# Sums of squares on GpSimd, half slabs of the context first, 64-row filter tiles and re-spread side slabs in a two-block fp32 kernel

## The reference, cut to what matters

```python
def rmsnorm(x, g):                        # ten norms of this kind, over the 1024 features
    xf = x.astype(jnp.float32)
    xf = xf * lax.rsqrt(jnp.mean(xf * xf, axis=-1, keepdims=True) + NORM_EPS)
    return xf.astype(x.dtype) * g
...
x = x + jnp.concatenate([y_attn, y_ssd, y_pool], axis=-1) @ w_out
h = rmsnorm(x, norm_ffn)
gate, up = jnp.split(h @ w_gate_up, 2, axis=-1)
return x + (jax.nn.silu(gate) * up) @ w_down            # then rmsnorm(x, norm_final)
...
def ffn_half(s, shift, scale, gate, g_pre, g_post, w_in, w_out):
    h = swiglu(modulate(rmsnorm_2(s, g_pre), shift, scale), w_in, w_out)
    return s + 0.5 * gate * rmsnorm_2(h, g_post)
...
# hyena_kernel: the filter net on 64 features, then (256x64) @ (64x2048), times a decay
h = jnp.sin(freq * (z @ w1 + b1))
h = jnp.sin(freq * (h @ w2 + b2))
h = jnp.sin(freq * (h @ w3 + b3))
h = (h @ w4).astype(f32)
```

## Time and profile before

| | us |
|---|---|
| median of 3 runs (lowest, highest) | 1420.91 (1420.67, 1421.95) |
| the profiled execution, whole | 1422.07 |
| its span in the trace | 1420.2 |
| PE busy in the span | 1321.3 |
| DVE, ACT, POOL busy | 865.0, 590.7, 58.1 |

### The profile page before, as it was taken

One profiled execution on the slowest core, in us unless ns is written; L12 is line 12 of the kernel. 1 busy time (PEld: TensorE's weight loads), 2 busy tenths in 40 slices (PEclk: granted clock), 3 DMA queues, 4 the chain that ended last, 5 costly groups with the idle time before them and its releaser, 6 DMA issues.

```text
span 1420.2 us, 20572 instructions
## 1 busy us (share of the span) xinstructions
PE 1321.3 (93%) x8392; PEld 1175.9 (83%) x8392; DVE 865.0 (61%) x1360; ACT 590.7 (42%) x942; POOL 58.1 (4%) x68
## 2 busy tenths in 40 slices
PE   6898799999699999999989899999899988899996
PEld 6887799998588888888766798778588987899996
DVE  4775677696878765554324794347766664555544
ACT  5564445444423232222213552236335634444542
POOL 0040000000000000000001430001000000000000
PEclk9999999999799999999989999999999998899998
DMA  6343277675355675566223153223223443355552
GB/s 253 121 148 119 96 233 225 208 240 177 124 186 192 191 230 194 181 203 204 83 78 111 53 167 108 89 96 128 74 75 100 143 152 127 106 188 182 173 173 71
DMA packets 60510, 213.02 MB, mean 150 GB/s; under 512 B 6608, under 2 KB 8784, under 8 KB 60160
## 3 DMA queue, kind: packets, MB, share of 16 engines
q1 hardware_dynamic: 58880, 205.55, 44.4%
q0 software_dynamic: 1248, 5.44, 1.1%
q10 hardware_dynamic: 288, 0.71, 0.1%
HBM read 210.63 MB, written 1.05 MB: 149 GB/s over the span
## 4 chain that ended last, share of the span: by engine, by line
PE 80%; DVE 10%; ACT 5%; issue 3%; DMA 1%; SPq 0%; POOLq 0%; POOL 0%; DVEq 0%; ACTq 0%
PE ps L1573 23%; PE ps L1575 22%; PE ps L1574 22%; ACT hi L482 3%; PE ps L1618 3%; DVE lo L962 2%; PE ps L1922 1%; PE ps L1609 1%; PE ps L1610 1%; PE ps L1611 1%; PE ps L1973 1%; PE ps L1886 1%; DVE rinv L984 1%; PE ps L1962 1%; PE ps L1941 1%
## 5 line engine op out<-in xcount | busy, mean ns | idle before, releaser
L1573 PE MATMUL ps<-nh,hi 128*128 128x256 f32 (+1 forms) x1936 | 611.6, 316 | 40.7 <-DVE lo L962 14.3
L962 DVE TENSOR_TENSOR lo<-raw,hi 128x1024 fp32r<-128x1024 f32 (+1 forms) x322 | 390.1, 1212 | 376.8 <-ACT hi L482 376.7
L1574 PE MATMUL ps<-nh,lo 128*128 128x256 f32 (+1 forms) x1936 | 599.0, 309 | 0.0
L1575 PE MATMUL ps<-nl,hi 128*128 128x256 f32 (+1 forms) x1936 | 598.8, 309 | 0.0
L482 ACT ACTIVATE hi<-raw 128x1024 fp32r<-128x1024 f32 (+1 forms) x322 | 334.6, 1040 | 504.9 <-PE ps L1575 469.1
L1573 PEld LDWEIGHTS ps<-nh,hi 128*128 128x128 f32 x1936 | 376.2, 194 | 75.4 <-issue 26.6
L1574 PEld LDWEIGHTS ps<-nh,lo 128*128 128x128 f32 x1936 | 377.2, 195 | 17.5 <-issue 0.5
L1575 PEld LDWEIGHTS ps<-nl,hi 128*128 128x128 f32 x1936 | 376.5, 194 | 16.3
L1573 PE MATMUL ps<-H,hi 128*128 128x256 f32 (+1 forms) x528 | 174.7, 331 | 0.3 <-DVE lo L962 0.3
L1574 PE MATMUL ps<-H,lo 128*128 128x256 f32 (+1 forms) x528 | 169.0, 320 | 0.0
L1575 PE MATMUL ps<-H,hi 128*128 128x256 f32 (+1 forms) x528 | 168.9, 320 | 0.0
(11 more groups left out here) (292 smaller groups left out, 991.5 us busy)
## 6 DMA issues: line engine op xcount, KB each, us to landing
raw<-in_up SPq DMA_DIRECT2D x132, 512.0 KB, 3.5
raw<-in_in SPq DMA_DIRECT2D x86, 512.0 KB, 3.3
raw<-in_w_ada SPq DMA_DIRECT2D x72, 512.0 KB, 4.2
raw<-in_down SPq DMA_DIRECT2D x48, 512.0 KB, 3.8
raw<-in_down SPq DMA_DIRECT2D x24, 384.0 KB, 3.1
raw<-in_out SPq DMA_DIRECT2D x8, 512.0 KB, 3.3
raw<-in_hy_out SPq DMA_DIRECT2D x8, 512.0 KB, 3.3
raw<-in_da_out SPq DMA_DIRECT2D x8, 512.0 KB, 3.3
```

The costliest lines, as they stand in the source:

```text
L962: dve.tensor_tensor(lo[:, h, 0:w], raw[:, r, 0:w], hi[:, h, 0:w].bitcast(F32), ALU.subtract).then_inc(lo_done, 1)
L1573: mm(o, hi[:, h, wk], x_hi, start=first, stop=False)
L1574: mm(o, lo[:, h, wk], x_hi, start=False, stop=False)
L1575: return mm(o, hi[:, h, wk], x_lo, start=False, stop=last)
```

## The change

- `TURNS` gets a semaphore `acc`. GpSimd's new `gather` adds the squares of tiles 0 to 6 or 0 to 7 of a norm, one 128x256 (or 128x512) addition for each tile after the first; PE then does one product with ones (`gathered`), and in most norms a second for the last tile (`last_square`), in place of eight. This holds for mix1, ffn1, pre2c, pre2x, post2, mod2c, post_mix2 and post3 (38 additions 256 wide, 12 of 512); mod2x and pre3 keep eight products. ACT's wait ahead of a square is now for `acc`. The places of the products move: mix1's behind slab 1 of in1, mod2c's to one place behind slab 7 of mixed, ffn1's and post_mix2's ahead of the last tile of their stage's last slab, pre2x's, post2's and post3's behind slab 22.
- The first three slabs of up2 are gone through twice on PE: first the context's 256 columns of all three, then those of x (`half_product`). The context's operands (pre2c) are made four slabs earlier in down1.
- The filter net's third layer is computed twice, on partitions 0 to 63 and 64 to 127; `w4` comes in one DMA of 128 rows, and the two products of a block take rows 0 to 63 and 64 to 127. The blocks stand behind slabs 13, 15, 18 and 20 of down2, their sums behind 15, 17, 20 and 22. In down2 ACT does `down_pair` ahead of `split`.
- `rides`: 12 in up1, 4 in down1, none in up2 until slab 6, then one behind each, two behind slabs 30 to 35, 12 in down2.
- The second half of x's load goes behind the first weight slab. In in1 many small steps move by a slab or so on all engines, and four of the small products become two. V's copies are shared by ACT and DVE, and PE waits for them later. In da_out, o2, out1, down1 and down3 the order of a `split` and the norm's steps beside it is turned round on ACT or DVE at the last slab.

The diff, cut to its core:

```diff
 TURNS = {
+    "acc": dict(mix1=6, ffn1=6, pre2c=7, pre2x=6, post2=6, mod2c=7, post_mix2=6, post3=6),
-    "stat": dict(mix1=8, ffn1=8, pre2c=8, pre2x=8, post2=8, mod2x=8, mod2c=8, post_mix2=8, pre3=8, post3=8),
+    "stat": dict(mix1=1, ffn1=1, pre2c=1, pre2x=1, post2=1, mod2x=8, mod2c=1, post_mix2=1, pre3=8, post3=1),
...
+            def gather(m, tiles, to, per=1):
+                for k in range(1, TURNS["acc"][m] + 1):
+                    pool.wait_ge(sem("sq"), since("sq", m) + per * (k + 1))
+                    if k > 1:
+                        pool.wait_ge(sem("acc"), since("acc", m) + k - 1)
+                    pool.tensor_tensor(to, tiles(0) if k == 1 else to, tiles(k), ALU.add)\
+                        .then_inc(sem("acc"), 1)
...
                 if k >= 4:
-                    act.wait_ge(sem("stat"), since("stat", m) + k - 3)
+                    if m in TURNS["acc"]:
+                        act.wait_ge(sem("acc"), since("acc", m) + max(1, k - 4))
...
             for x in st["o2"]:
-                split(x.s + HL)
                 down_one("post_mix2", x)
+                if x.j < KD - 1:
+                    split(x.s + HL)
             root("post_mix2")
+            split(x.s + HL)
...
             for x in st["down2"]:
-                split(x.s + HL)
                 if x.last:
                     down_pair(x)
-                if x.j in (14, 16, 18, 20):
-                    magnitudes((x.j - 14) // 2)
+                split(x.s + HL)
+                if x.j in (14, 16, 19, 21):
+                    magnitudes((14, 16, 19, 21).index(x.j))
...
+            def gathered(m, acc, o):
+                pe.wait_ge(sem("acc"), since("acc", m) + TURNS["acc"][m])
+                return mm(o, ones, acc, start=True, stop=TURNS["acc"][m] == 7)
+
+            def last_square(m, src, o, per=1):
+                pe.wait_ge(sem("sq"), since("sq", m) + per * KD)
+                mm(o, ones, src, start=False, stop=True).then_inc(sem("stat"), 1)
...
-            stat2("pre2x", KD - 1, 2)
+                if x.j == 22:
+                    gathered("pre2x", acc2[:, :], SUM2)
+            last_square("pre2x", sq2[:, 1, :], SUM2, 2)
...
-            for x in st["up2"]:
-                dense(x, slice(0, 2 * T), "pre2x" if x.j == 0 else None)
+            early = st["up2"][:3]
+            for x in early:
+                begin(x)
+                for k in range(KD):
+                    half_product(x, k, c_)
+            for x in early:
+                for k in range(KD):
+                    if x.j == 0:
+                        pe.wait_ge(sem("nl"), since("nl", "pre2x") + k + 1)
+                    m = half_product(x, k, x_)
+                m.then_inc(slab_used, 1)
+            for x in st["up2"][3:]:
+                dense(x, slice(0, 2 * T))
...
                 for n in range(2):
-                    o = mm(ps[:, 5 + n, :], filt3[:, tt * P:tt * P + P], w4[:, n, :], start=True, stop=True)
+                    rows = slice(64 * n, 64 * n + 64)
+                    o = mm(ps[:, 5 + n, :], filt3[rows, tt * P:tt * P + P], w4[rows, h, :], start=True, stop=True)
...
-                if x.j in (13, 15, 17, 19):
-                    filter_block((x.j - 13) // 2)
-                if x.j in (15, 17, 19, 21):
-                    filter_sums((x.j - 15) // 2)
-            stat2("post2", KD - 1, 1)
+                if x.j in (13, 15, 18, 20):
+                    filter_block((13, 15, 18, 20).index(x.j))
+                if x.j in (15, 17, 20, 22):
+                    filter_sums((15, 17, 20, 22).index(x.j))
+                if x.j == 22:
+                    gathered("post2", acc2[:, :], SUM2)
+            last_square("post2", sq2[:, 1, :], SUM2)
...
-                if 3 <= i <= 6:
-                    if i == 3:
-                        pe.wait_ge(sem("kf_copied"), 8)
-                    for k in (2 * i - 6, 2 * i - 5):
-                        stat("mod2c", k, sqd[:, k % 4, :], ps[:, 7, 0:T])
+                if i == 7:
+                    gathered("mod2c", rtd[:, :], ps[:, 7, 0:T]).then_inc(sem("stat"), 1)
...
-                    for tt in range(4):
+                    for tt in range(2):
                         act.activation(V[:, tt, o:o + 512], ps[:, tt, :], ACT.Copy).then_inc(bank_free[tt], 1)
```

More of the change, by code:

```diff
@@ L182, in plan @@
     rides = {}
-    for n in range(10):
-        rides["up1", 4 * n + 5] = n
-    for n in range(6):
-        rides["down1", 2 * n] = 10 + n
-    for n in range(44):
-        rides["up2", n] = N_EARLY + n
-    for n in range(12):
-        rides["down2", n] = 60 + n
+    for n in range(12):
+        rides["up1", 3 * n + 5] = [n]
+    for n in range(4):
+        rides["down1", 2 * n] = [12 + n]
+    n = N_EARLY
+    for j in range(6, 44):
+        more = 2 if 30 <= j < 36 else 1
+        rides["up2", j] = list(range(n, n + more))
+        n += more
+    for j in range(N_ADA - n):
+        rides["down2", j] = [n + j]
     uses, ring, w = [0] * BANKS, [], 0
@@ L196, in plan @@
         if (x.name, x.j) in rides:
-            ring.append(("ada", rides[x.name, x.j]))
+            ring += [("ada", n) for n in rides[x.name, x.j]]
         if x.name == "v2":
@@ L206, in plan @@
         if kind == "ada":
-            ring[g + 1][1].chunks.append((x, g))
+            y = next(y for kind, y in ring[g:] if kind == "weights")
+            y.chunks.append((x, g))
     return st, work, ring
@@ L240, in build @@
         idle = keep("idle", [P, 16])
+        acc2 = place(0, "acc2", [P, 2 * T])
         rinv = keep("rinv", [P, T])
@@ L368, in _, with load_x @@
         def _(sp):
-            for half in range(2):
+            def load_x(half):
                 w = slice(4 * half, 4 * half + 4)
                 sp.dma_start(xT[:, w, x_], d["x"][:, w, :]).then_inc(sem(f"x_landed{half}"), 16)
+            load_x(0)
             for g, (kind, x) in enumerate(ring):
@@ L690, in sines @@
                 act.wait_ge(sem("sin_arg"), n + 1)
-                act.activation(filt3[:, :], filt[:, 3, :], ACT.Sin).then_inc(sem("sin_ready"), 1)
+                rows = slice(0, P if n == 2 else 64)
+                act.activation(filt3[rows, :], filt[rows, 3, :], ACT.Sin).then_inc(sem("sin_ready"), 1)
             def final_squares(y):
@@ L698, in final_squares @@
                 if k >= 2:
-                    act.wait_ge(sem("stat"), since("stat", "pre2x") + k - 1)
+                    act.wait_ge(sem("acc"), since("acc", "pre2x") + max(1, k - 2))
                 act.activation(sq2[:, k % 2, 0:T], xT[:, k, x_], ACT.Square, scale=cols8[:, 1, k:k + 1])\
@@ L717, in _ @@
                     final_squares(st["down1"][x.j - 1])
-                if x.j >= 16:
-                    rounded("pre2c", xgc, x.j - 16, c_)
+                if 12 <= x.j < 20:
+                    rounded("pre2c", xgc, x.j - 12, c_)
             final_squares(st["down1"][-1])
+            split(st["down1"][-1].s + HL)
             root("pre2x", bias="eps_sq")
@@ L731, in down_pair @@
                 if k >= 2:
-                    act.wait_ge(sem("stat"), since("stat", "post2") + k - 1)
+                    act.wait_ge(sem("acc"), since("acc", "post2") + max(1, k - 2))
                 act.activation(sq2[:, k % 2, :], got(y), ACT.Square).then_inc(sem("sq"), 1)
@@ L1254, in angles @@
                 dve.wait_ge(sem("filt_pre"), l + 1)
-                x, t, y = filt[:, 0, :], filt[:, 1, :], filt[:, 2, :]
-                after(step(dve.tensor_scalar(x, ps[0:64, 5, T:2 * T], pc("filt_b", l)[0:64, :],
-                                             pc("filt_freq")[0:64, :], ALU.add, ALU.mult)))
+                rows = slice(0, P if l == 2 else 64)
+                x, t, y = (filt[rows, n, :] for n in range(3))
+                after(step(dve.tensor_scalar(x, ps[rows, 5, T:2 * T], pc("filt_b", l)[rows, :],
+                                             pc("filt_freq")[rows, :], ALU.add, ALU.mult)))
                 after(step(dve.tensor_scalar(t, x, 1.0 / two_pi, magic, ALU.mult, ALU.add)))
@@ L1679, in _ @@
                 m.then_inc(slab_used, 1)
-                if p < 1:
+                if p == 0:
                     pe.wait_ge(sem("con_landed"), 16)
-                    for k in range(KD):
-                        stat1("mix1", k)
-                if p == 4:
+                if p == 1:
+                    gathered("mix1", rinv[:, :], SUM1)
+                    last_square("mix1", sq[:, 3, :], SUM1)
+                if p == 5:
                     pe.wait_ge(sem("lam_prod"), 1)
@@ L1939, in values2 @@
                     pe.wait_ge(sem("otok_ready"), r)
+                else:
+                    for tt in range(4):
+                        pe.wait_ge(bank_free[tt], st["v2"][-1].uses[tt] + 1)
                 for kt in range(4):
@@ L1983, in turn_out @@
                 o.then_inc(sem("ott_ready"), 1)
-            for tt in range(4):
-                pe.wait_ge(bank_free[tt], st["v2"][-1].uses[tt] + 1)
             p = -1
@@ L2022, in _ @@
```

(6 more changed lines are left out.)

371 lines of the change are left out of this document (197 added, 174 removed).

## The result

The changed kernel takes 1395.27 us (median of 4 runs, 1392.52 to 1396.39) against 1420.79 before (1420.48 to 1421.95): ratio 0.9815, 95% interval 0.9801 to 0.983. It is 1.8% faster, but only 25.5 us of the 45 forecast arrived, and the time lies above the range's upper end of 1390. The profiled execution took 1396.39 us with a span of 1394.6, where 1377.3 was forecast: 19.1 us are missing.

What follows compares the result with a forecast made beforehand. PE, busy 93% of the span, was taken as the bound. Stage terms summed to -44.8 us from the profiled 1422.07, giving 1377.3, or 1376 for the median; forecast 1366 to 1384, range 1363 to 1390.

Steps and rivals of the forecast that it cites:

- start and in1: Program start and in1: earlier first slab load, fewer products in mix1, a later step and fewer small products; -6.6 us.
- out1: In out1, slabs without sums follow at 2.8 us, saving 5.7; a longer tail costs 1.1; -4.6 us in all.
- the tail of down1: From down1's slab 23 into up2: shorter wait for the last square, no gap, no low clock; -13.8 us.
- the trap at the end of out1: At out1's end, DVE's reciprocal waits behind lo, which waits for ACT's hi, put behind the root; +1.1 us.
- down1, -17.6: Down1 and start of up2: five of six sums leave the loop, -4.3 with 0.5 wait, and a shorter tail, -13.8.
- down2, -10.0: Down2: sums -4.3, filter blocks -5.2, sums behind the slow block 1.1 less, waits +1.1 with 0.5 of low clock.
- mixed, +3.7: Mixed: sums save 3.0, but PE waits 5.3 for GpSimd's late adds and pays 1.3 of low clock.
- Rival (b): GpSimd and DVE disturb each other, every add taking 1.60 us; +10, 1386 us; chance 0.18.
- v2, -3.5: Behind v2, sharing V's copies and waiting later cuts a 3.25 wait and 1.7 of low clock, leaving 1.5; -3.5 us.
- (a): The new waits charged in mixed, down2 and elsewhere do not arise, up to 11 us less; 1365 us; chance 0.14.
- (c): The filter net's 64-row tiles in down2 go one after the other; +3.6, 1380 us; chance 0.04.
- (d): GpSimd's adds come onto PE's path, slower than before, through ACT's squares and hi; 1456 us; chance 0.06.

Runs made afterwards that it cites:

- Opening the ring: Changed kernel with ACT's rounding and DVE's remainder of pre2c's tiles one slab later in down1, loosening the loop hi, lo, scaling, rounding, hi; 1383.49 us.
- best2: Changed kernel with all mends, down1's table load back at slab 11 and mod2c's reciprocal, rounding and remainders one slab earlier than in the first such kernel; 1366.51 us.
- The shifts: Changed kernel with four or eight unread products added on PE in up1, 1391.16 and 1397.94 us; four unread squares on ACT at the start, 1395.60 us.

## Why the prediction was wrong

- **What bounds the kernel; start and in1; out1; up1; the tail of down1; down3:** right. The first product of up1 came 11.25 us earlier (forecast 11.2), with 0.5 us of wait for the additions; the trap at the end of out1 was right as a mechanism, but its price was 2.1 us, not 1.1, since in the kernel before `hi` was made far ahead of the root and nothing of the 2.3 us was there yet. That out1 still came out at -4.7 (forecast -4.6) is luck: the rest of it gained 6.8 us where 5.7 was taken, so two errors of 1.1 and 1.0 cancel.
- **down1, -17.6, found -9.8.** The step that failed is "Five of the six sums in the loop go: 5 x 0.86 = -4.3, with 0.5 of wait". It took for granted that PE's own work paces the loop. With the sums a round of three slabs was 8.8 us against the ring's 9.0; without them PE would need 7.9, and GpSimd's additions made the ring 10.0. So in place of the sums' 4.3 us stand 5.9 us of waits for `lo` (0.3 before): 3.3 behind slab 14, which the ring makes, and 2.6 at slab 14. The last addition was waited for 2.2 us instead of 0.5. Opening the ring brings 6.1 of the 7.8 back. The wait at slab 14 is not explained by a run: it stays with additions of one column (2.3), with the ring open (2.6) and with the table load moved away (2.5). By the rows DVE has no idle time there between the filter net's steps, pre2c's gains and its reciprocal of 1.74 us, which the change makes earlier, and comes late to `lo`; the prediction counted what that move gains at the tail, and nothing for its place in the loop.
- **down2, -10.0, found -2.6.** The blocks (1.13) and the waits (8.0 for 8.1) were right. The step that failed is the term "with 0.5 of low clock": against best2, which has no spell in down2, the products of weights alone lost 5.7 us behind the waits, and those of filters and sums over 3, where the kernel before had one spell and lost 3.0 on the weights. The shifts show that 5 us of this belong to the place in time, not to the change: the same waits cost 166.2 or 171.0. The forecast of a fixed 0.5 was a number for a thing that has two values.
- **mixed, +3.7, found +6.6.** The mechanism was right and the wait 6.2 us, the top of the range of 4.4 to 6.4: six additions took 1.27 us each on end, where 0.81 to 1.1 was taken. Not in the sum was a wait of 1.2 us for `lo` two slabs before k2; it is there with additions of one column too, and not with the eight products on PE.
- **Rival (b)** had the right mechanism and a wrong place. It priced the additions' own length (1.60 each), which in mixed were 1.15 on average; in down1 the price fell on DVE's instructions, in a ring of 9.0 us a round that was already longer than PE's 7.9. With additions of one column 13 us go, where the rival had 10; but in the profiled execution of that kernel 4.9 us are down2's spells, so that the nearness of the two numbers says little.
- **v2, -3.5:** the wait fell by 2.2 us, from 3.25 to the 1.0 for V that stayed, and the low spell behind it, priced at 1.7, is gone; the table counts that spell in the woven stages. They gained only 1.6 all the same, among other things because the trap of `hi` and `lo` cost 2.1 us at post_mix2 too. Rivals (a), (c) and (d) didn't come.

The range was too narrow because the terms of low clock were taken as if they were known, at four places with 0.5 to 2.1 us each.

The Trainium skill, "SBUF — State Buffer", section "SBUF: two separate sides", says of the port pair of GpSimd and DVE that the one that is late is fully blocked. The scaling that took 1.50 us beside an addition of 1.61 and 0.48 without one agrees with that: DVE lost 1.0 us at once. The prediction worked out the rule's price on GpSimd's side only.

## What to carry to other kernels

Before work is taken off the bounding engine in a loop, measure the period of the other engines' ring in that loop, hand-overs included: the saving ends there, and a helper engine that shares ports lengthens exactly that ring. Where two engines pass a tile back and forth in one iteration, let the second step lag by an iteration. Put a gathered result where the helper is done, not where the data are, and where the helper is already late leave the work on the main engine.

## What the runs showed of the hardware

- The granted clock behind a wait of 2 to 3 us is not a function of the wait: four waits that are equal to 0.1 us were followed by three spells of 6.8 us at 0.5 or by one of 10.2, and the place in time decided it (down2 171.0, 166.2 and 171.2 us where it begins 0, 2.7 and 4.7 us later). A kernel's time can thus change by 4 us either way, 0.3%, by an edit that does no work; comparisons of less should go by stages and waits.
- A DVE instruction of 0.48 us with two inputs in SBUF took 1.50 beside a GpSimd addition of 512 columns, which itself took 1.61 in place of 1.29.
- Two products of 64 rows on either half of the rows took 1.13 us at full clock where two on the same half took 1.95.
